# Latent attention of a two-block layer: operands prepared channel by channel inside the gate panels, spilled as high and low parts, and loaded for 128-row score products

## What is computed

```python
q = (rmsnorm(c_q) @ w_uq).reshape(S, 8, 96)           # 64 plain + 32 rotary channels per head
q = concat([q[..., :64], rope(q[..., 64:])]) * 96**-0.5
kv = (rmsnorm(c_kv) @ w_ukv).reshape(S, 8, 128)        # 64 key channels + 64 value channels per head
k = concat([kv[..., :64], broadcast(rope(k_rope))])    # the rotary key is shared by the heads
p = softmax(q @ k.T)                                    # 1024 x 1024 for each of 8 heads, no mask
y_mla = ((p @ v) * silu(z_mla)) @ w_o_mla
```

## Time and profile before

| | us |
|---|---|
| median of 3 runs | 1885.41 |
| lowest, highest | 1879.91, 1885.81 |
| profiled execution | 1881.52 |
| its span, first to last instruction | 1879.7 |
| PE busy | 1776.3 (94%) |
| DVE, ACT, POOL busy | 822.0, 586.8, 476.8 |

### The profile page before, as it was taken

One profiled execution on the slowest core, in us unless ns is written; L12 is line 12 of the kernel. 1 busy time (PEld: TensorE's weight loads), 2 busy tenths in 40 slices (PEclk: granted clock), 3 DMA queues, 4 the chain that ended last, 5 costly groups with the idle time before them and its releaser, 6 DMA issues. The chain is left out here.

```text
span 1879.7 us, 22749 instructions
## 1 busy us (share of the span) xinstructions
PE 1776.3 (94%) x9048; PEld 1505.2 (80%) x9048; DVE 822.0 (44%) x1349; ACT 586.8 (31%) x1324; POOL 476.8 (25%) x330
## 2 busy tenths in 40 slices
PE   5999999999999989999999999999997999999998
PEld 4777777888777778799888998777776888887776
DVE  3240455447013054430454214422215899984723
ACT  4101455334100135300443104311113666661112
POOL 6114022054222110222002220203321333435320
PEclk9999999999999999999899999999998999999999
DMA  6113012342421010211002110244343012106332
GB/s 192 40 57 101 12 57 63 124 130 61 143 89 34 20 42 21 60 35 39 28 24 63 46 34 29 63 156 132 130 163 127 20 35 82 27 22 237 124 123 90
DMA packets 86666, 144.52 MB, mean 77 GB/s; under 512 B 25888, under 2 KB 35744, under 8 KB 86432
## 3 DMA queue, kind: packets, MB, share of 16 engines
q10 hardware_dynamic: 50800, 86.24, 13.4%
q1 hardware_dynamic: 35760, 56.81, 10.2%
HBM read 104.30 MB, written 38.73 MB: 76 GB/s over the span
## 5 line engine op out<-in xcount | busy, mean ns | idle before, releaser
L544 POOL TENSOR_SCALAR w_hi<-w_stage 128x1024 fp32r<-128x1024 f32 (+4 forms) x123 | 125.1, 1020 | 1111.1 <-PEq L882 524.1
L548 POOL TENSOR_TENSOR w_lo<-w_stage,w_hi 128x1024 fp32r<-128x1024 f32 (+4 forms) x123 | 266.1, 2168 | 9.3
L877 PE MATMUL ps<-w_hi,h2T_hi 128*128 128x512 f32 x584 | 251.7, 431 | 2.3 <-issue 1.6
L877 PE MATMUL ps<-w_lo,h2T_hi 128*128 128x512 f32 x584 | 238.5, 408 | 0.0
L877 PE MATMUL ps<-w_hi,h2T_lo 128*128 128x512 f32 x584 | 238.2, 408 | 0.0
L1891 DVE TENSOR_TENSOR rope_cos_part<-ps,cos_dil 128x512 f32<-128x512 f32 x48 | 33.2, 692 | 371.6 <-PE ps L877 294.0
L877 PEld LDWEIGHTS ps<-w_hi,h2T_hi 128*128 128x128 f32 x584 | 161.3, 276 | 16.3 <-issue 5.4
L877 PEld LDWEIGHTS ps<-w_lo,h2T_hi 128*128 128x128 f32 x584 | 162.6, 278 | 9.4
L877 PEld LDWEIGHTS ps<-w_hi,h2T_lo 128*128 128x128 f32 x584 | 161.4, 276 | 10.7
L569 PE MATMUL ps<-h2T_hi,w_hi 128*128 128x512 f32 x384 | 154.5, 402 | 5.8 <-ACT gate_tiles L1361 2.4
L569 PE MATMUL ps<-h2T_lo,w_hi 128*128 128x512 f32 x384 | 152.2, 396 | 0.0
(11 more groups left out here) (270 smaller groups left out, 3590.7 us busy)
## 6 DMA issues: line engine op xcount, KB each, us to landing
w_stage<-in_w_in SPq DMA_DIRECT2D x76, 512.0 KB, 3.7
w_stage<-in_w_out SPq DMA_DIRECT2D x16, 512.0 KB, 3.6
gate_scr<-gate_tiles ACTq DMA_DIRECT2D x16, 512.0 KB, 2.9
gates<-gate_scr ACTq DMA_DIRECT2D x32, 256.0 KB, 3.4
dil_scr<-dil_out ACTq DMA_DIRECT2D x24, 264.0 KB, 2.1
dil_nums<-dil_scr ACTq DMA_DIRECT2D x24, 256.0 KB, 4.0
x_tiles<-in_x ACTq DMA_DIRECT2D x8, 512.0 KB, 8.6
x_back<-in_x ACTq DMA_DIRECT2D x8, 512.0 KB, 3.7
```

Source lines behind the costliest of these rows:

```text
L544: last = nc.gpsimd.tensor_scalar(hi_, raw_, 1.0, 0.0, ALU.mult, ALU.add)
L548: last = nc.gpsimd.tensor_tensor(lo_, raw_, hi_.bitcast(F32), ALU.subtract)
L877: m = pe.matmul(ps[:, u % 2, :], toks(a, k), b[:, s, k, :], start=(k == 0 and b is wh and a is h2h), stop=(k == KT - 1 and a is h2l))
```

## The change

The weights of mla are moved ahead of zd in the order of panels. POOL sorts them while splitting: plain query channels of all heads, first and second rotary halves of all heads, key channels, value channels (16 pieces in 3 chunks instead of 3). A list `PREP` of 40 units runs on PE between gate units 4 to 12, on PSUM banks 4 to 7:

```diff
+    JOINT_LAG, JOINT_STEP = 6, 2
+    PREP = ([("c", n, kind) for n in range(HALF) for kind in range(3)] + [("c", n, 3) for n in range(HALF)]
+            + [("t", i, n) for i in range(2) for n in range(HALF)]
+            + [("n", j, n) for j in range(4) for n in range(HALF)]
+            + [("r", n, a) for n in range(HALF) for a in range(2)]
+            + [("k", j, n) for j in range(4) for n in range(HALF)] + [("v", t, 0) for t in range(TT)])
+    PREP_AT = {4: range(0, 3), 5: range(3, 6), 6: range(6, 8), 7: range(8, 22), 8: range(22, 24),
+               9: range(24, 29), 10: range(29, 34), 11: range(34, 38), 12: range(38, 40)}
...
         for u in range(16):
...
             gate_unit(u)
+            for x in PREP_AT.get(u, ()):
+                prep_unit(x)
```

```diff
+        def prep_after(u):
+            for x in PREP_AT.get(u, ()):
+                prep_high(x)
+                y = stage_of.get(x, 0)
+                if y:
+                    stage_spill(staged[y - 1])
+        gate_evac(range(2, 16), gt, prep_after)
```

For the loop SP loads, from the spilled parts, V (4 MB, after the last joined tile), head 0 (18 DMAs), head 1 (16, once the last gate is done), and each later head (14, once the head before the last has been scored). Head inputs are not made in the loop. The scores:

```diff
-            for n in range(HALF):
-                m = three_passes(ps[:, 2 * (i % 2) + n, :], [
-                    (Qh[:, h % 2, P * qt:P * qt + P], Ql[:, h % 2, P * qt:P * qt + P],
-                     Kh[:, h % 2, COLS * n:COLS * n + COLS], Kl[:, h % 2, COLS * n:COLS * n + COLS])])
+            Q, K, q = heads_q[h % 2], heads_k[h % 2], slice(P * qt, P * qt + P)
+            for part in range(2):
+                for n in range(HALF):
+                    pe.matmul(ps[:, 2 * (i % 2) + n, :], Q[:, part, q], K[:, part, COLS * n:COLS * n + COLS],
+                              start=(part == 0), stop=False)
+            for n in range(HALF):
+                rows = slice(MLA_R * n, MLA_R * n + MLA_R)
+                m = pe.matmul(ps[:, 2 * (i % 2) + n, :], Q[rows, 2, q], KC[rows, :], start=False, stop=True)
```

In the loop the output of a pair of steps goes through three engines, with two PSUM banks (6 and 7) in place of one:

```diff
-            in_turn(nc.vector.tensor_copy(dst, ps[HD:P, 6, 0:256]))
-            in_turn(nc.vector.tensor_tensor(dst, ps[0:HD, 6, 0:256], dst, ALU.add))
-            nc.vector.tensor_tensor(dst, dst, zm[0:HD, b % 2, :], ALU.mult).then_inc(sem("m_out"), 1)
+            act.activation(am[0:HD, b % 2, :], ps[HD:P, 6 + b % 2, 0:256], ACT.Copy).then_inc(sem("m_half"), 1)
...
+            nc.vector.tensor_tensor(dst, ps[0:HD, 6 + b % 2, 0:256], dst, ALU.add).then_inc(sem("m_added"), 1)
...
+            nc.gpsimd.tensor_tensor(dst, dst, zm[0:HD, b % 2, :], ALU.mult).then_inc(sem("m_out"), 1)
```

More of the change, by code:

```diff
@@ L516, in dil_split, with split_high, split_low @@
                 nc.gpsimd.tensor_scalar(hi, hi.bitcast(F32), 1.0, 0.0, ALU.mult, ALU.add).then_inc(sem("dil_hi"), 1)
+        def split_high(n, parts):
+            pool.wait_ge(*after(f"w_landed{n % STAGE}", 16 * (n // STAGE + 1)))
+            for raw_, hi_, _ in parts:
+                last = nc.gpsimd.tensor_scalar(hi_, raw_, 1.0, 0.0, ALU.mult, ALU.add)
+            last.then_inc(sem("w_high"), 1)
+        def split_low(n, parts, end=True):
+            pool.wait_ge(*after("w_high", n + 1))
+            for raw_, hi_, lo_ in parts:
+                last = nc.gpsimd.tensor_tensor(lo_, raw_, hi_.bitcast(F32), ALU.subtract)
+            if end:
+                last.then_inc(sem("w_split"), 1)
@@ L530, in _ @@
             if p >= 2:
                 pool.wait_ge(*after("panel_used", p - 1))
-            for k, cols, src in chunks:
-                raw = stage[:, n % STAGE, :, 0:cols]
+            split = []
+            for ci, (k, cols, src) in enumerate(chunks):
+                raw = stage[:, (n + ci) % STAGE, :, 0:cols]
                 hi = wh[:, p % 2, k:k + CHUNK_K, 0:cols]
@@ L1036, in m_transposes @@
                     pe.wait_ge(*after("m_lo", 2 * i - 1 + half))
+                elif half == 0:
+                    pe.wait_ge(*after("dg_done", TT))
                 for j in range(4):
@@ new lines, in _, with stage_half @@
+        act.wait_ge(*after("tables", 4))
+        for i, w in enumerate((C_Q, C_KV)):
+            act.activation(c_ss[:, i, :], c_ss[:, i, :], ACT.Sqrt, scale=1.0 / w, bias=EPS_C).then_inc(sem("c_root"), 1)
+        def stage_half(x, low):
+            slot = spare[:, stage_of[x] % SLOTS, :]
+            kind = PREP[x][0]
+            if kind == "v":
+                return slot.rearrange("p (h a c) -> p h a c", a=2, c=HD)[:, :, low, :]
+            rows = slice(0, MLA_R if kind == "c" else P)
+            return slot[rows, COLS * low:COLS * low + COLS]
@@ new lines, in stage_spill @@
+        def stage_spill(x):
+            kind, i, n = PREP[x]
+            slot = spare[:, stage_of[x] % SLOTS, :]
+            halves = slot.rearrange("p (a s) -> p a s", a=2).bitcast(F32)
+            if kind == "r":
+                act.wait_ge(*after("q_rope_low", prep_count("r", x) + 1))
+                src, dst = halves, qr_d[:, n, :, COLS * i:COLS * i + COLS].rearrange("a p s -> p a s")
+            else:
+                act.wait_ge(*after("prep_read", x + 1))
+                if kind == "c":
+                    src, dst = halves[0:MLA_R], kr_d[:, :, COLS * i:COLS * i + COLS].rearrange("a p s -> p a s")
+                elif kind == "v":
+                    src, dst = slot.bitcast(F32), v_d[P * i:P * i + P, :]
+                else:
+                    rows = (qn_d, kn_d)[kind == "k"][:, P * i:P * i + P, COLS * n:COLS * n + COLS]
+                    src, dst = halves, rows.rearrange("a p s -> p a s")
+            act.dma_start(dst, src).then_inc(sem(f"stage_out{stage_of[x] % SLOTS}"), 16)
@@ L1880, in _ @@
+        for x, (kind, _, a) in enumerate(PREP):
+            if kind != "r":
+                prep_low(x)
+            elif a == 0:
+                rope_pair(x)
         phase_end(dve, "dve")
```

622 lines of the change are left out of this document (342 added, 280 removed).

## The result

The changed kernel takes 1864.51 us (median of 4 runs, 1862.42 to 1865.84) against 1884.0 us for the kernel before on the same chip (4 runs, 1879.91 to 1885.81): ratio 0.9904, 95% interval 0.9888 to 0.9919. It is faster, by 19 us where 45 were forecast, and lies 4.5 us above the range. The profiled execution takes 1865.84 us with a span of 1864.0.

What follows compares the result with a forecast made beforehand. The loop was taken as bound by PE and DVE, DVE slightly ahead. From 1881.5 us, -49.5 + 33.1 - 2.4 + 4.6 - 30.1 = -44.3 gave 1837.2, plus half of 3.9: 1839; range 1826 to 1858, plus 2 for the runs.

Steps and rivals of the forecast that it cites:

- preparation in the gate panels: First gates: products of 27.9 us and transposes of 5.2 us added to PE, +33.1; first-evacuation pause gone, -2.4; waits, +4.6.
- added waits of 4.6: First gates: PE waits for table scalings (2.6 us) and stage slots (2 us), +4.6 us, bounds 1 and 14.
- the spills: Rival, first gates: slots or zd's late chunks stall PE in units 7 to 12; 1848 us, chance 0.12.
- The sum: Loop: 64 steps of 3.1 us plus 1.5 for filling, 199.9 us, a gain of 30.1 us.
- the sentence on ACT's order: Loop: ACT's output copy, ahead of the high parts, waits only for values already done; ACT 2.72 us a step, below PE's.
- I take the pair as one product: Loop: two 32-row score products at different rows overlap and cost 0.233 us, making PE's step 2.99 us instead of 3.22.
- together not: Rival, loop: the two 32-row products do not overlap, six products stay six in time; 14.9 us longer, 1854 us, chance 0.17.
- the 0.1 a step for hand-offs: Loop: 0.1 us a step added to PE's pieces, as in the kernel before, giving 3.1 us a step.
- the filling of the pipeline: Start of the loop: PE has gaps while the pipeline fills, 1.5 us added to 198.4.
- VectorE's 2.92: Loop: DVE's work falls to 2.92 us a step, no longer ahead of PE.
- hand-offs bind the loop: Rival, loop: four engines at 90% in fixed order, a step of 3.4 us; 19 us longer, 1858 us, chance 0.11.
- The tail: After the loop: PE nearly full, nothing to win; zero change, bounds -1.5 and +3 us.

Runs made afterwards that it cites:

- repeated runs: The changed kernel and both parts run again, nothing edited, on another chip than their first runs: 1867.01 us and 1847.85 us.
- full rows: Changed kernel with each pair of 32-row products replaced by two 128-row products against zero-padded keys, two output slots: 1866.07 us, loop 225.3 us.
- no pair: Changed kernel without the two 32-row score products, two output slots: 1857.84 us in one run, loop 225.4 us.
- same-rows run: Changed kernel with three output slots and both 32-row products reading rows 0 to 31: 1869.54 us in one run, loop 224.5 us.
- both parts: Changed kernel with two zero-padded 128-row products for each 32-row pair, and four output slots: 1836.65 us, loop 200.8 us.

## Why the prediction was right or wrong

**Right: what is gained before the loop.** There is no gap behind gate 47 but 0.26 us of idle time. The timeline of PE there:

```profile
1440.39 0.40 PE L696 MATMUL ps<-h2T_hi,w_lo 128*128 128x512 f32 x1
1441.05 1.17 PE L1156 MATMUL ps<-k_mla,q_mla 128*128 128x512 f32 x4 [0.26 <-issue]
```

The forecast had the first score at 1439.5. The preparation in the gate panels was to cost 35.3 us; the stage to the first dilated product ends 31.0 later (545.4, then 576.4), with PE busy 123.95 of 126.60. The added waits of 4.6 did not come (below the lower bound of 1): ACT waits for slots for up to 2.27 us there, but PE's banks carry it over them. Neither the spills nor zd's late chunks bound, so that rival falls. The 4.3 us won on the forecast there went again in the dilated stage, 5.1 us longer (652.9 and 658.0 us). The mean granted clock there is 0.974 and 0.966; time multiplied by clock is 636 us either way, so the clock is enough to account for all of it. The repeated runs show that it differs from run to run.

**Wrong: the loop, in three terms.** The sum had 199.9 us and the trace 228.6. The experiments split the 28.7: 15.1 are the stores (226.0 to 210.9), 10.1 the pair against two full products (210.9 to 200.8), and 3.5 are left even so: six full products for the five of the sum, less the hand-offs and the filling that did not come. A head takes 28.5 us (1494.2 to 1522.7), where over 26 was named as the sign of being wrong.

First, and largest, the sentence on ACT's order: "The copy stands ahead of the high parts in ACT's order and waits for values of the step before, done by then." That names one wait of two. The copy into `a_mla` also waits for the landing of the store that last used the slot, which went out only one step before. I had followed the store forward to what it waits for, and not back to who waits for its landing. It costs 15.1 us (226.0 to 210.9), of which PE's seven pauses are 10.9, and while it stands nothing that relieves PE shows in the total (full rows: 225.3; no pair: 225.4). The kernel before kept the output path on DVE and stored four steps ahead of the slot's next use, beside little traffic: a DMA share of 0.14 in its loop, 0.44 after. The ring has two slots in both. What the change brought are the late store and the loads of 2 MB a head. The two are needed together: without the head loads the loop takes 211.0 us with two slots, and with the loads it takes 210.9 with three.

Second, "I take the pair as one product": 0.23 us for what is 0.64 in PE's time (3.39 a step less the 2.75 of its other pieces) and 0.41 in the loop's. The overlap that I argued for is there (0.21 a step, by the same-rows run). The mis-sized term is what surrounds it: weight loads of 32 rows behind a full product, and of 128 rows behind the pair, are not started ahead, and the load unit stands idle for 23.8 us before the pair in 64 steps. By starts it costs 0.09 in the scores ahead of the pair and 0.12 in the values behind it. The rows that I went by (64-row scores, which follow one another for eight products) never switch inside the pack. The trace before held a sign of the price where such a pack begins: the last of eight transposes of 128 rows starts at 700.25 us and the pack at 700.45, 0.20 us later, while the transposes are 0.11 apart. (Eight in turn would have been 1.92 us by the 0.22 given, not 1.88; nothing hangs on it.) The rule I cited, the Trainium skill's TensorE: Matmul & The Clock Gate, Part 3, "The mechanism", also says that a load overlaps running products only where its row group differs. With full-array products as neighbours that is a rule against this change, and I should have weighed it; the trace agrees for the pair, though not for the 128-row loads, which overlap here (1490.78 above). Against two full products the pair costs 10.1 us instead of saving 14.9. That is dearer than the rival *together not* had it (0.64 for 0.47), though the overlap which that rival denies is there.

Third, going the other way: the 0.1 a step for hand-offs. With PE the bound it is busy 99% and a step is its pieces, 3.21 for 3.19 measured (200.8 over 63). Nor did the filling of the pipeline cost 1.5 us: the first steps have fewer pieces, and 64 x 3.21 is 205.4 for 203.4 measured. The loop of both parts, 200.8 and 2.6 to the mixer, is 3.5 us above the forecast with all six products in it. VectorE's 2.92 held: by the changed kernel's durations it is 2 x 0.678 + 1.214 + 0.164 + half of 0.417, 2.94.

The rival *hand-offs bind the loop* gave a step of 3.4, against 3.39 in the middle of a head. That is chance. It named four engines at 90% and no wait for a DMA, and ACT is busy 66%.

**The tail** came out 1.8 us shorter, just beyond the lower bound of 1.5.

**Open.** Whether the exposed load belongs to the change of row count itself or to the position of the rows: no run placed a 32-row product among others of 32 rows. How much of the 15.1 us is the clock was not separated by a run. The granted clock is 0.93 in 1550 to 1600 us of the changed kernel, where PE pauses, which is 3.5 us of 50 at most. What the kernels with two slots would take if their pauses did not lower the clock is open too.

## What to carry to other kernels

When work moves to another queue, list for every instruction behind it all its waits, back to the landings: a buffer ring is long enough only against the landing time that the new traffic makes, here 4 to 6 us where the median is 2. Before you put a small pack of products between full-array ones, price the change of shape on both sides: here a pair of 32 rows lost to two products padded with zeros. And where two costs sit on different limits, undo them together as well as one by one: alone, the better products were worth nothing in total, and with the third slot 10 us. A total that does not move can hide a gain in most steps and a loss in a few.

## What the runs showed of the hardware

Two 32-row products at different rows take 0.43 us from start to next start, at the same rows 0.66, and two of 128 rows 0.47. Around a 32-row pair the array loses about 0.2 us more: the loads before (0.37 idle) and behind it (0.25) are not started ahead.

A 64 KB store that lands in a median of 1.9 us took up to 5.8 us in the changed kernel's loop; the long ones fall together with the reading of a head's 2 MB on SP's queue, the longest also with that of the dilated operand on ACT's.

The granted clock of the dilated stage differs between executions of one program: 0.97 in 780 to 984 us of one execution of both parts, 0.92 in another, with PE busy 192.53 us in each. The first score of the changed kernel and its variants came between 1430.0 and 1450.3 us. Differences of less than some 10 us between whole kernels need the stage's own window beside them.
